# A two-layer transformer trunk on one core: six weight slots where there were four

## The reference, cut to what matters

```python
for layer in range(2):
    m = pool_nsa_mixer(x, ...) if layer == 0 else rglru_mixer(x, ...)
    x = layer_norm(ALPHA * x + m, ...)
    c = memory_cross_attention(x, mem, x_wq, x_wkv, x_wo)
    x = layer_norm(ALPHA * x + c, ...)
    f = (silu(h[:, :2816]) * h[:, 2816:]) @ w_down        # h = x @ w_up
    x = layer_norm(ALPHA * x + f, ...)
```

## Time and profile before

| | us |
|---|---|
| median of three runs | 1537.52 |
| lowest, highest run | 1534.15, 1537.78 |
| the profiled execution, its own time | 1531.01 |
| its span in the profile | 1529.2 |
| PE busy within the span | 1501.4 (98%) |
| DVE, ACT, POOL busy | 547.6, 611.0, 667.1 |

### The profile page before, as it was taken

How to read it: one execution, slowest core, us unless ns; L and a number is a source line. 1 busy time by engine, 2 the same in 40 slices (tenths; PEclk the granted TensorE clock), 3 DMA queues, 4 the chain that set the end, 5 groups by cost and what they waited for, 6 DMA issues and landing times.

```text
span 1529.2 us, 21541 instructions
## 1 busy us (share of the span) xinstructions
PE 1501.4 (98%) x7906; PEld 1268.4 (83%) x7906; DVE 547.6 (36%) x918; ACT 611.0 (40%) x1222; POOL 667.1 (44%) x530
## 2 busy tenths in 40 slices
PE   8999999999999999999999999999999999999998
PEld 7889998888888888888887867788888888888886
DVE  2753555454372101110006188845444111011014
ACT  3345554344443323332233468734433333233221
POOL 5542122532455444444464543554243444444442
PEclk9999999999999999999999999999999999999999
DMA  9331112321234333333232522332122332333222
GB/s 240 94 97 55 33 39 80 110 97 56 90 95 143 92 103 97 97 91 103 97 121 86 152 80 66 109 118 97 56 90 97 97 98 89 105 97 99 97 97 90
DMA packets 115714, 147.05 MB, mean 96 GB/s; under 512 B 20534, under 2 KB 74160, under 8 KB 115632
## 3 DMA queue, kind: packets, MB, share of 16 engines
q1 hardware_dynamic: 115312, 145.87, 31.0%
q0 software_dynamic: 320, 0.08, 0.0%
HBM read 143.80 MB, written 2.10 MB: 95 GB/s over the span
## 4 chain that ended last, share of the span: by engine, by line
PE 93%; DVE 3%; ACT 2%; issue 1%; DMA 0%; POOL 0%; SPq 0%; DVEq 0%; ACTq 0%
PE ps L648 83%; PE ps L873 3%; PE ps L653 2%; PE ps L853 2%; PE ps L837 1%; DVE h L1705 1%; DMA x_res<-in_x 0%; PE ps L798 0%; DVE h L1731 0%; PE ps L930 0%; POOL w_lo L612 0%; PE ps L829 0%; DVE ib_alt L1730 0%; DVE h L1738 0%; ACT ra L1314 0%
## 5 line engine op out<-in xcount | busy, mean ns | idle before, releaser
L612 POOL TENSOR_TENSOR w_lo<-w_raw,w_hi 128x512 fp32r<-128x512 f32 (+2 forms) x468 | 601.4, 1293 | 833.2 <-ACT w_hi L1073 830.3
L1073 ACT ACTIVATE w_hi<-w_raw 128x512 fp32r<-128x512 f32 (+2 forms) x468 | 280.4, 612 | 549.1 <-PE ps L648 539.1
L648 PE MATMUL ps<-fm_hi,w_hi 128*128 128x512 f32 (+1 forms) x1112 | 423.2, 381 | 7.2 <-POOL w_lo L612 5.3
L648 PE MATMUL ps<-fm_lo,w_hi 128*128 128x512 f32 (+1 forms) x1112 | 420.0, 378 | 0.0
L648 PE MATMUL ps<-fm_hi,w_lo 128*128 128x512 f32 (+1 forms) x1112 | 419.9, 378 | 0.0
L648 PEld LDWEIGHTS ps<-fm_hi,w_hi 128*128 128x128 f32 x1112 | 210.0, 189 | 48.6 <-POOL w_lo L612 7.3
L648 PEld LDWEIGHTS ps<-fm_lo,w_hi 128*128 128x128 f32 x1112 | 210.1, 189 | 38.7 <-issue 0.7
L648 PEld LDWEIGHTS ps<-fm_hi,w_lo 128*128 128x128 f32 x1112 | 209.8, 189 | 38.9
L1866 DVE TENSOR_TENSOR gf<-silu,ps 128x512 f32<-128x512 f32 x44 | 28.3, 684 | 417.4 <-ACT silu L1406 399.7
L1613 DVE SCALAR_TENSOR_TENSOR x_res<-x_res,ps 128x512 f32<-128x512 f32 x48 | 31.4, 686 | 273.1 <-PE ps L648 187.8
L648 PE MATMUL ps<-w_hi,g_hi 128*128 128x512 f32 x288 | 112.0, 389 | 0.0
(11 more groups left out here) (280 smaller groups left out, 2213.5 us busy)
## 6 DMA issues: line engine op xcount, KB each, us to landing
w_raw<-in_f_w_up SPq DMA_DIRECT2D x352, 128.0 KB, 2.1
w_raw<-in_f_w_down SPq DMA_DIRECT2D x88, 256.0 KB, 2.6
w_raw<-in_x_wkv SPq DMA_DIRECT2D x48, 256.0 KB, 3.1
w_raw<-in_o_w_in SPq DMA_DIRECT2D x40, 256.0 KB, 2.6
w_raw<-in_x_wq SPq DMA_DIRECT2D x32, 256.0 KB, 2.7
w_raw<-in_x_wo SPq DMA_DIRECT2D x32, 256.0 KB, 2.8
w_raw<-in_e_w_in SPq DMA_DIRECT2D x24, 256.0 KB, 2.9
w_raw<-in_o_w_out SPq DMA_DIRECT2D x20, 256.0 KB, 2.6
```

Of the source, the lines that this page charges most:

```text
L612: nc.gpsimd.tensor_tensor(lo[:, :n], w_raw[:, c % RING, :n], hi[:, :n].bitcast(F32), ALU.subtract).then_inc(w_split, 1)
L648: last = nc.tensor.matmul(outp, lhsT, rhs, start=(clear and k == 0 and n == 0), stop=(k == steps - 1 and n == 2), skip_group_check=True)
L1073: nc.scalar.activation(w_pair(c)[0][:, :n], w_raw[:, s, :n], ACT.Copy).then_inc(w_rounded, 1)
```

## The change

`RING` becomes 6. The low part gets no slots of its own any more: `w_lo` is laid over `w_raw`, so POOL overwrites the raw weights with their low part (for a held chunk the low part still goes to its own place). Memory is unchanged: twice six slots take the space of three times four. Because PE now reads the low part out of the raw slot, SP may load into that slot only when PE has used the old chunk, and only behind a held chunk is the split enough.

A new constant `LAST` = 4 stays where 4 meant "the last four chunks" or "four early chunks". At a norm with a following product, PE runs four half-width chunks before tile 3 and two behind it, and the wait for tile 3 is put in two parts: all but the last copy before the product, the last copy at chunk 4. The first filler is cut in two, with the transposes of tile 3 between its chunks 0 to 3 and 4 to 7. ACT's rounding at the norms and in the recurrence is arranged anew for the longer ring. All up-projection loops are written out.

```diff
-RING = 4
+RING = 6
+LAST = 4
...
-        w_raw, _ = place("w_raw", [P, RING, COLS], F32)
+        w_raw, o_raw = place("w_raw", [P, RING, COLS], F32)
+        w_lo = at("w_lo", [P, RING, COLS], F32R, o_raw)
         w_hi, _ = place("w_hi", [P, RING, COLS], F32R)
-        w_lo, _ = place("w_lo", [P, RING, COLS], F32R)
...
                 for c in range(first, last):
                     if c >= RING:
-                        sp.wait_ge(w_split, c - RING + 1)
+                        sp.wait_ge(w_split if c - RING in HELD_OF else w_used, c - RING + 1)
...
                 turn_normed(l, i, 2)
                 if following:
                     evacuated(f"ln{l}{i}_0")
-                    early_half(following, 0, RING - 1)
+                    early_half(following, 0, LAST)
                 for name, feature_major in fillers[:1]:
-                    product(name, mem, MEM, feature_major)
+                    product(name, mem, MEM, feature_major, chunks=(0, LAST))
                 turn_normed(l, i, 3)
                 if following:
-                    early_half(following, RING - 1, RING)
+                    early_half(following, LAST, RING)
+                    evacuated(f"ln{l}{i}_1", but=1)
+                for name, feature_major in fillers[:1]:
+                    product(name, mem, MEM, feature_major, chunks=(LAST, KT))
                 for name, feature_major in fillers[1:]:
                     product(name, mem, MEM, feature_major)
-                evacuated(f"ln{l}{i}_1")
+                if not following:
+                    evacuated(f"ln{l}{i}_1")
+
+            def last_tile_turned(l, i):
+                return lambda k: evacuated(f"ln{l}{i}_1") if k == KT // 2 else None
...
-                round_weights(following + RING - 1)
+                round_weights(following + LAST - 1)
                 deviation(2)
                 if turns:
                     turned_copies(1)
-                round_weights(following + RING)
+                round_weights(following + LAST)
                 if turns:
                     turned_copies(2)
                 deviation(3)
-                if fillers:
-                    round_weights(following + KT + RING - 1)
+                round_weights(following + RING)
                 if turns:
                     turned_copies(3)
...
                             nc.scalar.activation(RA[n][:, j, :], RA[n][:, j, :], ACT.Exp,
                                                  scale=lru_c[:, 1, first + j:first + j + 1]).then_inc(decay_ready, 1)
+                            if j == tiles // 2 - 1:
+                                round_on(1, meanwhile)
```

More of the change, by code:

```diff
@@ L664, in _, with product @@
             mem = (mem_hi, mem_lo)
-            def product(name, act, tokens, feature_major, col0=(0, P, 2 * P, 3 * P), ready=None, order=None, early=0, m=0,
+            def product(name, act, tokens, feature_major, col0=(0, P, 2 * P, 3 * P), ready=None, order=None, early=0,
                         by_tile=None, chunks=None):
-                b0, steps = 4 * (INDEX[name] % 2) if early or (chunks and chunks[0]) else begin(name, m), PLAN[INDEX[name]][1]
+                b0, steps = 4 * (INDEX[name] % 2) if early or (chunks and chunks[0]) else begin(name), PLAN[INDEX[name]][1]
                 hi, lo = act
@@ L751, in _ @@
             evacuated("x0")
-            early_half("ein0", 0, RING)
+            early_half("ein0", 0, LAST)
             evacuated("x1")
-            product("ein0", fm, SEQ, True, early=RING)
+            product("ein0", fm, SEQ, True, early=LAST)
             pe.wait_ge(s_mem, 16)
@@ L937, in _ @@
                     recurrence_gates(0)
-                    product("oin2", fm, SEQ, True, chunks=(0, KT - RING))
+                    product("oin2", fm, SEQ, True, chunks=(0, KT - LAST))
                     o2, c2 = 4 * (INDEX["oin2"] % 2), CHUNK0["oin2"]
                     for i, j in enumerate(OIN2_BANKS):
-                        for k in range(KT - RING, KT):
+                        for k in range(KT - LAST, KT):
                             if i == 0:
@@ L961, in _ @@
                     turn_late(0, 0, "q0_0")
-                product(f"q{l}_0", fm, SEQ, True, early=RING)
+                product(f"q{l}_0", fm, SEQ, True, early=RING, ready=last_tile_turned(l, 0))
                 name = f"q{l}_1"
@@ L1044, in _ @@
                     turn_late(0, 1, fillers=(("k1_0", True), ("k1_1", True)))
-                for n in range(UP_FIRST):
-                    product(f"up{l}_{n}", fm, SEQ, True, early=0 if n else RING * l)
-                with pe.Fori(0, UP_PAIRS) as m:
-                    for n in (UP_FIRST, UP_FIRST + 1):
-                        product(f"up{l}_{n}", fm, SEQ, True, m=m)
+                for n in range(FT // 2):
+                    product(f"up{l}_{n}", fm, SEQ, True, early=0 if n else RING * l,
+                            ready=last_tile_turned(1, 1) if l and not n else None)
                 product(f"dn{l}_0", (g_hi, g_lo), SEQ, False, ready=lambda k: pe.wait_ge(g_ready, l * FT + k + 1))
```

103 lines of the change are left out of this document (31 added, 72 removed).

## The result

| | before | after |
|---|---|---|
| median of the runs | 1537.5 us | 1551.8 us |
| lowest to highest | 1534.2 to 1537.8 | 1549.4 to 1558.1 |
| the profiled execution: time, span | 1531.0, 1529.2 us | 1550.9, 1549.1 us |
| mean granted clock of its span | 0.997 | 0.994 |

The ratio is 1.0115, 95% interval 1.0083 to 1.0147: the change makes the kernel 14 us slower by the medians, 19.9 us by the two profiled executions. The forecast was 1559.0, range 1546 to 1571.

A forecast was written before the change was run, and what follows sets the result against it. PE's instruction stream plus its stops bound the kernel (PE busy 1501.4 of 1529.2 us). Terms +15.7 +10.1 +3.6 -2.7 -1.4 -3.8 = +21.5 on 1531.0 gave 1552.5; 6.5 more for the median gave 1559.0, range 1546 to 1571.

The forecast's parts named there:

- part 1: Six held groups, tile 0: PE waits for held chunks reloaded late, 2.6 us a group, +15.7 us.
- Part 2: Opening: `mem_tok` and chunk 12 go out and land later, so `ein0`'s copies and `ein1` are late; with half clock +10.1 us.
- Rival (a): Opening: the queue drains in time, chunk 12 lands at 36.4, costing 0.7 us; time 1549.6 us, chance 15%.
- The prediction's own sign of being wrong: PE's waits for POOL under 6 us in sum, or `pool_in` copied before 40 us in the opening.
- Parts 3 to 6: Copies waiting for a landing +3.6 us; fillers -2.7; three norms with a following product -1.4; recurrence -3.8.
- part 6: Recurrence: rounding ahead removes PE's 7.8 us loss, but ACT's late copy of the first gates leaves -3.8 us.
- At nothing: Written-out loops, low part over the raw one, and cross attention cost nothing; if the cover is wrong, about 1 us each layer.
- From the sum to the median: Whole kernel: 6.5 us added to the profiled execution's forecast of 1552.5, giving a median of 1559.0 us.
- The sum: Whole kernel: all terms added, +21.5 us on the profiled 1531.0, giving 1552.5 us for a profiled execution.

The follow-up runs named there:

- direct: Changed kernel, but a held chunk's transfer lands straight in the place where it is held; median 1536.0 us, ratio 1.0014 to the kernel before.
- again: The changed kernel run once more with no edit; median 1555.8 us, ratio 1.0136 to the kernel before.
- copyfirst: Changed kernel, but up to attention ACT rounds only three chunks beyond a group before its copies, not five; median 1544.9 us, ratio 1.0070 to the kernel before.
- latesets: Changed kernel, but compression and pooling weights' transfers come six chunks later in SP's order; median 1549.4 us, ratio 1.0087 to the kernel before.
- both: Changed kernel with the edits of direct and copyfirst together; median 1524.2 us, ratio 0.9949 to the kernel before.

## Why the forecast was right, and where it was not

The direction and the mechanism of part 1 held, and the time, 1551.8, was inside the range, 7 us under the forecast of 1559.0.

**Part 1: right in its geometry, too small in size.** The chain of 4.85 us measured 4.90 in `eout1`, the three waits forecast as 1.4, 0.6 and 0.6 were 1.33, 0.35 and 0.43 by the waits and 1.5, 0.5 and 0.65 from start to start, and `direct` took all of it away. The waits make 17 to 18 us in six groups, not 15.7: the last two chunks land 1.3 to 1.5 us apart, slower than POOL's 1.26 us, which I had taken for their pace. (The chunks that wait are 5 to 7, the sixth to the eighth; the fifth, which the prediction names too, was in time in all six groups.) The other 3 to 5 us is a term that I left out: half clock behind the stalls. I had given it to the opening alone, as if only a pause of 2.9 us brought it; behind the held groups' pauses of 1.3 and 0.4 us it came in three groups of six, in the second execution in one.

**Part 2: the step that failed.** I had read that the queue was the bottleneck with at most 2 us of slack, and carried its 21.8 us over. It was not. SP's issues in the kernel before, a row that I had not weighed:

```profile
17.05 0.73 SPq L517 DMA_DIRECT2D cmp_w<-in_e_cmp_wk  x1
23.21 1.74 SPq L473 DMA_DIRECT2D w_raw<-in_e_w_in  x2
```

Between 17.8 and 23.2 us SP itself stood still, for the split of a chunk that ACT rounded at 21.18, and so the set was stretched by its issues. With its issues closer together the same set took 16.2, 18.2 and 20.6 us in three executions. The gap (`after`, `again`, `direct`) was thus 4.0, 6.0 and 8.4 us long, 3.3, 5.3 and 7.7 more than before, where I forecast 8.4 more: right only for the slowest of them. The 1.7 us for the clock was 1.7 in the first and about 3 in the others. That the copies' place in ACT's order turns this landing into a gap is shown twice: `copyfirst` moves the copies, `latesets` the landing, and each takes away most of it. Rival (a), chunk 12 at 36.4 and `pool_in` copied before 40 us, is what the first profile nearly shows (36.9, and 37.5 to 39.5); the later ones lie between (a) and my number or near the latter. The prediction's own sign of being wrong, `pool_in` copied before 40 us, thus came true in the first profile, and the median lies nearer to (a)'s 1549.6 than to 1559.0.

The Trainium skill, page "DMA: Bandwidth & Descriptors", gave 11 us for the set. The page states its fit for single transfers issued from GpSimd; those here are issued by SP, several at a time. The 16.2 to 20.6 us measured without SP's pause show that the fit does not carry over to this set. In `latesets` one `cmp_w` transfer of 512 KB, with rows of 256 bytes, took 5.0 us with one 256 KB chunk beside it:

```profile
cmp_w<-in_e_cmp_wk SPq DMA_DIRECT2D x1, 512.0 KB, 5.0
```

By the fit of the Trainium skill's page it would be an estimated 3.2 us. Its section "Specifications" asks for 512 bytes or more, and this row agrees with that; no run here tried wider rows, so the cause is not shown.

**Parts 3 to 6** came within 1 us each: +2.8 for +3.6, -3.6 for -2.7 (the fillers' late chunk costs 0.4 us, not 0.7 and 1.0), -1.9 for -1.4, -3.0 for -3.8. But of these 3.0 us 1.7 is half clock that the profiled execution of before had at 915.8 us and this one had not. In `again`, `direct`, `copyfirst` and `both`, each with such a stretch of 3.4 us there, the stage gained 1.1 to 1.6 us; part 6 had counted the clock as a sure gain. In the recurrence what is late next is what part 6 named, ACT's order; the trace after shows the rounding in front of the sigmoids for which PE waits until 944.2:

```profile
937.74 2.71 ACT L1043 ACTIVATE w_hi<-w_raw 128x512 fp32r<-128x512 f32 x5
...
941.76 2.42 ACT L1261 ACTIVATE ra_alt<-ps,chan 128x512 f32<-128x512 f32 x4
```

**At nothing**: right for the loops and the subtraction.

**From the sum to the median: wrong.** The sum gave 1552.5 for a profiled execution, and that took 1550.9. But I added 6.5 us because the kernel before had so much between its profiled execution and its median. That distance was a good execution of before, no property of the program: after, it is 0.9 us, and over all later runs of the kernel before its medians were 1533.3 to 1535.8. 5.6 of the 7.2 us by which the forecast was too high are this step. In the sum itself the errors of parts 1 (7 too little) and 2 (5 too much) and of the start (2) nearly cancelled: that it came within 1.6 us of the profiled execution is luck.

## What to carry to other kernels

When a buffer's release moves from an early event to a late one, don't ask whether the mean rate still suffices but look for the place where the consumer passes through many buffers faster than one refill takes: here 0.68 us a chunk against 4.9 us. The space saved may still pay if the data of just that place land elsewhere: with held chunks in their own place and the opening's copies at their old place in ACT's order (`both`), six slots in the space of four are a gain of 0.5%. A deeper ring also lets a hand-ordered engine run further ahead; each wait for a landing that thereby comes in front of a copy must be counted as well.

## What the runs showed that I had not expected

- Half clock (1.2 GHz) after short stalls, and not in every execution. Behind `eout1`'s two longer stalls (1.5 and 0.5 us) the clock was 0.5 for 3.4 us in one execution of the changed kernel and 1.0 in the other, where they were 1.6 and 0.4 us. In `latesets` it lasted 6.8 us there:

```profile
303.20:310.00 6.80, 5.60 (x14) 4.33 (x14) 3.52 (x7) 2.18 (x4) 2.21 (x2) 0.52 0.35 114
```

  Over four executions with these stalls (both of the changed kernel, `copyfirst`, `latesets`) the six groups lost 20.1 to 26.8 us, and most of that spread is the clock.
- The same transfers in the same order take different times. Chunk 12, 256 KB behind a `cmp_w`, took 5.5, 7.1 and 9.5 us from issue to landing in three executions (`after`, `again`, `direct`), and 2.6 us where no `cmp_w` stood in front of it.
- Three 256 KB transfers issued within 0.9 us landed 2.6, 3.6 and 4.6 us after their issue: a burst of reloads is paced by the transfers, not by the engines that work on them.
